# Prompt attention of a hybrid trunk step: the softmax factors go into the turn of the probabilities, as a diagonal

## What is computed

```
s = jnp.einsum('btgrd,btgnd->btgrn', q, rows[..., 0, :]) * ATTN_SCALE
p = masked_softmax(s, mask)
return jnp.einsum('btgrn,btgnd->btgrd', p, rows[..., 1, :]).astype(q.dtype)
...
return gates[..., 0, None] * o_cmp + gates[..., 1, None] * o_sel + gates[..., 2, None] * o_win
```

## Time and profile before

| | us |
|---|---|
| time, median of 3 runs | 3086.37 |
| lowest and highest of them | 3079.68, 3093.54 |
| the profiled execution's own time | 3092.72 |
| its span, first to last instruction | 3090.9 |
| mean granted TensorE clock | 0.953 |
| busy: PE, DVE, ACT, POOL | 2815.1, 1126.4, 784.3, 258.0 |
| busy in line 1198 (POOL, 128 instructions) | 136.3 |

### The profile page before, as it was taken

How to read it: one execution, slowest core, us unless ns; L and a number is a source line. 1 busy time by engine, 2 the same in 40 slices (tenths; PEclk the granted TensorE clock), 3 DMA queues, 4 the chain that set the end, 5 groups by cost and what they waited for, 6 DMA issues and landing times.

```text
span 3090.9 us, 50695 instructions
## 1 busy us (share of the span) xinstructions
PE 2815.1 (91%) x21103; PEld 2599.9 (84%) x21103; DVE 1126.4 (36%) x1606; ACT 784.3 (25%) x1174; POOL 258.0 (8%) x243
## 2 busy tenths in 40 slices
PE   4999999996788687669999999999999999999998
PEld 3549999996666543449989999999999999999998
DVE  2322222226444553664433333233333333333333
ACT  1223111114344230142322122221222222122233
POOL 0000000000366101320100000000000000000002
PEclk9999999997799898679999999999999999999999
DMA  5135323322000554222222322223222222222222
GB/s 193 55 110 171 95 88 95 88 68 73 1 1 1 186 191 157 69 91 87 89 82 89 95 88 90 93 88 95 88 93 90 89 95 88 95 88 91 92 88 89
DMA packets 251880, 287.14 MB, mean 93 GB/s; under 512 B 21549, under 2 KB 244139, under 8 KB 247814
## 3 DMA queue, kind: packets, MB, share of 16 engines
q1 hardware_dynamic: 249214, 239.99, 25.0%
q0 software_dynamic: 2592, 46.14, 3.9%
HBM read 273.68 MB, written 20.71 MB: 95 GB/s over the span
## 4 chain that ended last, share of the span: by engine, by line
PE 80%; DVE 8%; POOL 4%; issue 2%; ACT 2%; DMA 2%; SPq 0%; ACTq 0%; POOLq 0%; DVEq 0%
PE PS L610 67%; POOL prob L1198 4%; PE PS L382 4%; DMA seg_raw<-in_cache_kv_cmp,idx_c 1%; PE PS L1100 1%; DVE c_tmp L1665 1%; DMA win_t<-kvs_tok 1%; PE PS L1370 1%; DVE seg_ord L464 1%; PE PS L368 1%; PE PS L1334 1%; DVE st_s L1901 1%; PE PS L1859 1%; PE PS L998 0%; PE PS L997 0%
## 5 line engine op out<-in xcount | busy, mean ns | idle before, releaser
L597 DVE TENSOR_TENSOR w_lo<-w_raw,w_hi 128x1024 fp32r<-128x1024 f32 (+1 forms) x388 | 460.3, 1190 | 1387.7 <-ACT w_hi L591 1386.7
L591 ACT ACTIVATE w_hi<-w_raw 128x1024 fp32r<-128x1024 f32 (+1 forms) x388 | 395.5, 1024 | 1501.1 <-PE PS L610 1501.1
L610 PE MATMUL PS<-h_hi,w_hi 128*128 128x260 f32 x3360 | 675.7, 283 | 7.4 <-DVE w_lo L597 5.1
L610 PE MATMUL PS<-h_lo,w_hi 128*128 128x260 f32 x3360 | 675.5, 283 | 0.0
L610 PE MATMUL PS<-h_hi,w_lo 128*128 128x260 f32 x3360 | 674.3, 282 | 0.0
L610 PEld LDWEIGHTS PS<-h_hi,w_hi 128*128 128x128 f32 x3360 | 516.6, 189 | 8.3 <-issue 7.5
L610 PEld LDWEIGHTS PS<-h_lo,w_hi 128*128 128x128 f32 x3360 | 519.3, 189 | 0.0
L610 PEld LDWEIGHTS PS<-h_hi,w_lo 128*128 128x128 f32 x3360 | 518.3, 189 | 0.0
L610 PE MATMUL PS<-u_hi,w_hi 128*128 128x260 f32 x2048 | 411.6, 282 | 8.4 <-DVE u_lo L2246 8.4
L610 PE MATMUL PS<-u_lo,w_hi 128*128 128x260 f32 x2048 | 410.8, 282 | 0.0
L610 PE MATMUL PS<-u_hi,w_lo 128*128 128x260 f32 x2048 | 410.3, 282 | 0.0
(11 more groups left out here) (384 smaller groups left out, 2580.7 us busy)
## 6 DMA issues: line engine op xcount, KB each, us to landing
w_raw<-in_w_up SPq DMA_DIRECT2D x256, 256.0 KB, 2.8
w_raw<-in_w_down SPq DMA_DIRECT2D x256, 256.0 KB, 2.9
w_raw<-in_w_in SPq DMA_DIRECT2D x160, 256.0 KB, 2.9
w_raw<-in_w_out SPq DMA_DIRECT2D x64, 256.0 KB, 3.1
out_kv_win_s<-in_state_kv_win SPq DMA_DIRECT2D x8, 1022.0 KB, 7.4
win_t<-in_state_kv_win SPq DMA_DIRECT2D x16, 448.0 KB
xtok<-in_x_prompt SPq DMA_DIRECT2D x4, 1024.0 KB, 9.2
x_r<-in_x_prompt SPq DMA_DIRECT2D x4, 1024.0 KB, 6.2
```

The costliest lines, as they stand in the source:

```text
L591: ins = e.activation(hi, raw, ACT.Copy)
L597: ins = e.tensor_tensor(lo, raw, hi.bitcast(F32), ALU.subtract)
L610: mm = e.matmul(PS[:, bank + 2 * m + h, 0:HN], w, x[:, k0 + k, h * HN:h * HN + HN], start=st and c == 0, stop=sp and c == 2)
```

## The change

`factors` now also builds, for each query tile, a 128x128 diagonal `diag_f` from the identity and the tile's factors, on VectorE, and signals `as_sc`. The turn is an ordinary matmul: the block of `prob` is the stationary operand as before, and the moving operand is `diag_f` in place of the identity, so that the turned block comes out scaled. `att_pool` is gone. There is one buffer of diagonals, so building them waits until the turn of the unit before is through (`as_T`). The wait of the factors for `as_sc` is dropped.

```
--- before.py
+++ after.py
@@ -874,6 +874,7 @@
         den = at("den", [P, 2, 4], SB + 2016)
         fac = at("fac", [P, 2, 4], SB + 2048)
         rec = at("rec", [P, 2, 4], SB + 2080)
+        diag_f = at("diag_f", [P, 4, P], 1536)
         cmx, cden, crec, cfac = (at(n, [P, 2, 16], SB + 2112 + 128 * z) for z, n in enumerate(("cmx", "cden", "crec", "cfac")))
         q_smp = at("q_smp", [P, 8, NB], SB + 2624)
         kc_hh = at("kc_hh", [P, NKV, 32], SB + 2880, F32R)
@@ -1097,8 +1098,8 @@
                         c0 = 384 if kt == 3 else 0
                         for qt in range(kt, 4):
                             c = P_OFF[qt] + kt * P
-                            last = e.transpose(PS[:, 4 + n, c0 + (qt - kt) * P:c0 + (qt - kt) * P + P],
-                                               prob[:, u % 2, c:c + P], ident[:])
+                            last = e.matmul(PS[:, 4 + n, c0 + (qt - kt) * P:c0 + (qt - kt) * P + P],
+                                            prob[:, u % 2, c:c + P], diag_f[:, qt, :], start=True, stop=True)
                     last.then_inc(as_T, 1)
 
             def values(u):
@@ -1161,9 +1162,13 @@
                 e.wait_ge(as_exp, 4 * (u + 1))
                 ch.step(e.reciprocal(rec[:, u % 2], den[:, u % 2]))
                 ch.settle()
-                if u >= 2:
-                    e.wait_ge(as_sc, 4 * (u - 1))
                 e.tensor_tensor(fac[:, u % 2], rec[:, u % 2], gv[:, h, 1 + b, :], ALU.mult).then_inc(as_fac, 1)
+                e.wait_ge(as_fac, u + 1)
+                if u:
+                    e.wait_ge(as_T, 3 * u)
+                for qt in range(4):
+                    e.tensor_scalar(diag_f[:, qt, :], ident[:], fac[:, u % 2, qt:qt + 1], None,
+                                    ALU.mult).then_inc(as_sc, 1)
 
             def head_out(h):
                 e.wait_ge(as_pv, 2 * (h + 1))
@@ -1189,14 +1194,6 @@
                     head_out(u // 2 - 1)
                 turned(u)
             head_out(NH - 1)
-
-        def att_pool(e):
-            for u in range(NU):
-                e.wait_ge(as_fac, u + 1)
-                for qt in range(4):
-                    p = prob[:, u % 2, P_OFF[qt]:P_OFF[qt] + (qt + 1) * P]
-                    e.tensor_scalar(p, p, fac[:, u % 2, qt:qt + 1], None, ALU.mult).then_inc(as_sc, 1)
-
 
         PV_ORDER = (6, 7, 0, 1, 2, 3, 4, 5)
         NS = 4
@@ -2374,7 +2371,6 @@
             const2_pool(e, ch)
             q_pool(e)
             values_pool(e)
-            att_pool(e)
             smp_pool(e, ch)
             ssd_pool(e, ch)
             out_pool(e)
```

More of the change, by code:

```diff
@@ L1191, in att_dve @@
             head_out(NH - 1)
[L1193 to L1198, removed]
         PV_ORDER = (6, 7, 0, 1, 2, 3, 4, 5)
```

## The result

| | before | changed |
|---|---|---|
| median of 7 runs, us | 3086.23 | 3069.70 |
| lowest to highest | 3079.68 to 3098.91 | 3066.65 to 3074.42 |
| profiled execution's span | 3090.9 | 3071.5 |
| busy POOL | 258.0 | 121.6 |

The ratio is 0.9945, with a 95% interval from 0.9925 to 0.9964: 16.5 us less in the medians. Two repetitions beside other kernels gave 0.9944 (0.9926 to 0.9962) and 0.9937 (0.9918 to 0.9956).

A forecast was written before the change was run, and what follows sets the result against it. The prediction took a loop through GpSimd to bound the attention stage, with TensorE right beneath. Gains of 8.1 us from second turn to next stage and 1.0 at the start made 9.1, from 3086.37 to 3077.3 us, range 3066 to 3090.

The forecast's parts named there:

- its best sum: Largest gain in the forecast's own range: 13.2 us, with turns of 2.12 us and 2.0 us gained at the start.
- the 7 us taken off for the runs' spread: Half-spread of the runs, put below the likelier part of the case's 3073 to 3091, giving 3066 to 3090.
- What binds: Attention stage: the loop through GpSimd, 6.91 us a unit, gives way to TensorE without waits, 6.19 or 7.08 us.
- the 4% of the chain: GpSimd's scaling pass in the whole span's chain of waits: some 130 us, which the forecast said was not all winnable.
- T: Duration of one unit's turn on TensorE, 20 matmul instructions with the diagonal: 2.22 us, between 2.12 and 2.65.
- Scores: TensorE's score matmuls in each attention unit, issued between turn and values: 1.76 us a unit.
- The start: Attention stage's start: first turn 3.1 us earlier but 4.4 us long at half clock; gain 1.0 us, at most 2.0.
- Diagonals at nothing: Four diagonals a unit on VectorE cost nothing in the steady state, covered by TensorE's work by over 1.5 us.
- Gathers at nothing: Sample stage's gathers, reached earlier by POOL's queue without the pass: no gain and no cost.
- The rest moves up as a whole: Everything behind the attention stage moves up as a whole, since the chain goes from the last values into the sample stage.
- more than expected: Rival: clock rises earlier and gathers landed sooner relieve loads; 13.2 us plus 3 or more later, 3070 us; chance 0.08.
- The chances: Forecast 0.76, rivals 0.24; by outcome: faster by over 0.5% 0.15, within 0.5% 0.75, slower 0.10.

The follow-up runs named there:

- The held turn: Changed kernel with only the attention stage's first turn held back until GpSimd ran four instructions of the old pass's size (4.3 us) on an unread buffer: 3078.8 us, ratio 0.9973.
- plain transposes: Changed kernel with diagonals still built, but turns done as transposes with the identity, leaving the probabilities unscaled: 3036.4 us, ratio 0.9832.

## Why the prediction was right, and where it was off

The forecast was 3077.3 us in a range of 3066 to 3090; measured were 3069.7, inside it. The median before had moved only to 3086.23, so it is 16.5 us of gain against 9.1 forecast. Of the 7.4 between them 5.1 lie in the stage, 2.3 in its steady part and 2.8 at its start, and the rest behind it. The forecast's own range ended at 3073, and its best sum was 13.2 us; the stage alone gave 14.25. So the result is inside the range only by the 7 us taken off for the runs' spread: the mechanism held, the size was too small, and some of the agreement is luck.

- **What binds.** A loop through GpSimd before, TensorE's own work after, with units of 6.2 and 7.1 us in turn: shown, at 6.12 and 7.01 us. That most of the 4% of the chain would not come back held too: 14 of 130 us did.
- **The turn's price.** T = 2.22 us from line 1117's spacing; it was 2.155. The spacing was right (2.40 us less the 0.275 of one instruction, over 19: 0.112), but from the last instruction of a turn to the first score there are only 0.03 us, where I had counted a whole spacing; 31 x 0.065 = 2.0 us.
  The factor of 4 that "TensorE: Matmul & The Clock Gate", section Terms, of the Trainium skill gives the transpose mode for FP32 was not met: an estimate by it is 4.24 us a turn; here it is 2.155 / 1.01, a factor of 2.1. "Perfetto Trace Analysis", section Transposes, was nevertheless right to want a transpose: with transposes and the pass on VectorE the kernel is 32 to 36 us faster than with the matmul.
- **Scores** took 1.75 instead of 1.76, some 0.3 us in sum. At the end the values waited 1.03 us for the copies (999.49 + 2.155 to 1002.67), 1.05 forecast. With the turn that makes 8.1 forecast and 10.4 measured between second turn and next stage.
- **The start** was the term that failed in size: 1.0 us forecast, with 2.0 as its end, 3.8 measured. I had the turn 3.1 us earlier and then gave nearly all of it back to ten doubled instructions at half clock. The turn took 3.31 us instead of 4.4, the scores 1.73 instead of 3.2, the values 2.21: the clock rose by 804, while that turn was running. That it may rise sooner was in the text, but with 2.0 us as its most. The held turn shows the other case.
- **Diagonals at nothing**: shown for the steady units, with at least 0.9 us of further cover and less than 2.7.
- **Gathers at nothing**: shown.
- **The rest moves up as a whole**: it did on average, but not rigidly. Two stretches move by up to 5 us with the clock and by up to 10 us with transfers and unnamed idle time. The rival "more than expected", 3070 us, named the earlier clock rightly and the gathers wrongly, and is where the result fell.
- **The chances.** Within 0.5% had 0.75, faster by more 0.15 (the parts named add up to 0.74 and 0.16). Three comparisons gave 0.55, 0.56 and 0.63% with intervals of 0.36 to 0.82. The gain is most likely just over the line. I was too sure: a sum of 9 us whose start could only be bounded loosely left more than 0.15 on that side of 15.4.

## What to carry to other kernels

Read, before an engine is relieved, how much slack the next one has per round: here 1.44 us by the prediction's count, under a pass of 4.27, and the replacement spent 1.1 of it on the engine that binds next. Work put on the engine that binds next was paid in full here, work put on one with cover cost nothing: the same scaling was free on VectorE and took 36 us on TensorE. A stage's first rounds deserve their own count, since an idle stretch taken away there also brings the clock forward.

## What the runs showed of the hardware

- A 128x128 f32 matmul was two instructions 0.112 us apart, a 128x128 f32 transpose one, 0.109 us from the next: at a granted clock of 1.00 a turn of ten was 2.155 us (changed kernel) against 1.01 (plain transposes, and the pass on VectorE).
- One and the same stretch of matmuls ran at a granted clock of 0.50 to 0.65 in one kernel and at 1.00 in another: 18.4, 17.8 and 18.4 us against 13.4, 13.6 and 14.0 in three executions of each, though the code and the waits for VectorE were the same.
- Where TensorE stood still before the stage's first turn, the granted clock went to 1.00 later: 7.1 to 10.6 us behind the factors in six profiles, 3.7 to 4.3 in the eight where it hardly stood.
- Elementwise instructions on SBUF slowed each other across GpSimd and VectorE: side by side, 603 became 1014 ns on GpSimd and 481 became 595 ns on VectorE.
